# Prompt attention in a hybrid decoder step: making the next pair's queries, keys and first scores inside the running pair

## The reference, cut to what matters

```
q = (c_q @ w_q_up)                      # 512 -> 16 heads x 96, then rope on the last 32
kv = (c_kv @ w_kv_up)                   # 256 -> 16 heads x (64 keys, 64 values)
for blk in range(L // Q_BLOCK):         # 4 blocks of 128 queries
    s = (q_nope . k_nope + q_pe . k_pe) * scale
    mask = pos[q0:q1, None] >= pos[None, :q1]
    p = softmax(where(mask, s, -inf))
    outs.append(p @ v[:, :q1])
# decode: q_lat = q_nope @ w_uk; scores against a paged cache of latents and rotary keys
# S5: products of the powers of a_bar with b_bar and c, used by the chunked scan
```

## Time and profile before

| | |
|---|---|
| median of 3 runs | 1593.4 us |
| lowest, highest | 1583.5, 1593.82 us |
| profiled execution, first to last instruction | 1590.6 us |
| first query product to the last values product | 79.3 to 314.5 us |
| TensorE: busy with matmuls, with weight loads | 94%, 89% of the span |
| VectorE, ScalarE, GpSimd busy | 49%, 38%, 22% |

### The profile page before, as it was taken

The page is one execution under the profiler, slowest core; times in us unless marked ns, Lnnn a source line. Parts: engine busy times, 40 slices in busy tenths (PEclk is TensorE's granted clock), DMA queues, the critical chain, the costliest instruction groups (busy, mean ns, idle before and its releaser), DMA issues.

```text
span 1590.6 us, 32114 instructions
## 1 busy us (share of the span) xinstructions
PE 1497.3 (94%) x11463; PEld 1418.5 (89%) x11463; DVE 772.5 (49%) x1234; ACT 603.5 (38%) x1085; POOL 356.2 (22%) x422
## 2 busy tenths in 40 slices
PE   5978998889999999999999998789999999999997
PEld 5966676688887999999999998789999999999997
DVE  3876656555553543442334454964444423344332
ACT  6444545475553333311233333342333311233233
POOL 0286776344310002200022132000012200122000
PEclk9999999999999999999999999889999999999998
DMA  7123323333433123223232565512222232222321
GB/s 178 24 59 87 100 79 101 111 97 91 116 91 116 55 84 88 79 85 87 71 87 79 179 153 159 191 35 80 79 80 79 79 93 79 80 79 85 87 67 60
DMA packets 245283, 147.62 MB, mean 93 GB/s; under 512 B 42072, under 2 KB 239615, under 8 KB 244191
## 3 DMA queue, kind: packets, MB, share of 16 engines
q1 hardware_dynamic: 237826, 138.35, 30.1%
q0 software_dynamic: 6704, 7.20, 1.8%
q10 hardware_dynamic: 684, 1.18, 0.2%
HBM read 128.42 MB, written 18.26 MB: 92 GB/s over the span
## 4 chain that ended last, share of the span: by engine, by line
PE 85%; DVE 8%; ACT 3%; issue 3%; DMA 1%; SPq 0%; ACTq 0%; DVEq 0%
PE bank L856 62%; PE bank L776 7%; PE bank L1114 3%; PE bank L1079 3%; PE bank L919 2%; PE bank L979 2%; PE bank L936 1%; PE bank L967 1%; DVE arena L2050 1%; DVE tmpa L2339 1%; ACT arena L1375 1%; DVE arena L2366 1%; DVE sq L2339 1%; DVE tmpa L2048 1%; DVE tmpa L2047 1%
## 5 line engine op out<-in xcount | busy, mean ns | idle before, releaser
L856 PE MATMUL bank<-arena_parts,wR 128*128 128x288 f32 x4224 | 566.0, 296 | 4.2 <-ACT arena_parts L1452 3.7
L856 PEld LDWEIGHTS bank<-arena_parts,wR 128*128 128x128 f32 x4224 | 562.9, 188 | 5.2 <-issue 4.9
L856 PE MATMUL bank<-side_parts,wR 128*128 128x288 f32 x3360 | 447.3, 295 | 1.1 <-DVE tmpa L2411 1.1
L856 PEld LDWEIGHTS bank<-side_parts,wR 128*128 128x128 f32 x3360 | 445.5, 188 | 1.5 <-issue 1.3
L1859 DVE TENSOR_TENSOR wR<-wraw,wR 128x1024 fp32r<-128x1024 f32 x159 | 232.8, 1464 | 241.5 <-ACT wR L1438 240.1
L741 POOL TENSOR_TENSOR arena_parts<-sq,arena_parts 128x576 f32 x64 | 91.6, 1431 | 729.8 <-ACT arena_parts L1669 729.8
L1438 ACT ACTIVATE wR<-wraw 128x1024 fp32r<-128x1024 f32 x159 | 167.0, 1050 | 202.0 <-PE bank L856 187.5
L1375 ACT ACTIVATE arena<-bank 128x256 f32<-128x256 f32 (+9 forms) x223 | 95.3, 443 | 135.0 <-PE bank L776 87.9
L1666 ACT ACTIVATE tmpa<-bank 128x576 f32<-128x576 f32 x64 | 41.7, 651 | 195.5 <-PE bank L856 195.5
L2262 DVE TENSOR_TENSOR sq<-tmpa 128x576 f32<-128x576 f32 x64 | 48.5, 759 | 127.2 <-ACT tmpa L1666 127.2
L2190 DVE TENSOR_TENSOR kpR<-bank,rstd 128x576 f32<-128x576 f32 x32 | 24.2, 758 | 127.9 <-PE bank L856 127.9
(11 more groups left out here) (300 smaller groups left out, 1604.6 us busy)
## 6 DMA issues: line engine op xcount, KB each, us to landing
wraw<-in_mlp_w SPq DMA_DIRECT2D x128, 512.0 KB, 4.0
side<-in_cache_ckv SPq DMA_DIRECT2D x128, 128.0 KB, 2.1
wraw<-in_ssm_w_glu SPq DMA_DIRECT2D x16, 512.0 KB, 4.0
s_state_to_out<-side SPq DMA_DIRECT2D x16, 256.0 KB, 2.5
s_in_to_state<-yblk SPq DMA_DIRECT2D x8, 512.0 KB, 2.6
s_in_to_out<-side SPq DMA_DIRECT2D x64, 64.0 KB
wraw<-in_mla_w_o SPq DMA_DIRECT2D x8, 512.0 KB, 5.2
side<-s_in_to_state SPq DMA_DIRECT2D x2, 2048.0 KB, 13.2
```

The costliest lines, as they stand in the source:

```text
L856: return pe.matmul(bank[:, a, 0:HALF], wR[:, s, wp, k, :], tokens(k, xp)[:, a * HALF:(a + 1) * HALF], start=(first and j == 0), stop=(last ...
```

## The change

Two sets of queries and keys now exist, chosen by the parity of the pair: the second query buffer lies in `sq`, the second key buffers in `acc` and `side`. The third score bank becomes half of `bank45`, and banks 6 and 7 (`bank67`) become helpers in which everything else of a pair is made, one thing after the other. Inside pair p, TensorE now makes the query product of head 0 of pair p+1 after the values of units 0 and 1, that of head 1 after the values of units 2 and 3, the keys of p+1 after the transposes of unit 5, and the scores of units 0 and 1 of p+1 around the last transposes of p. The values product, the up-projection's transposes and the latent queries stay at the pair's start; `chunk_lags` moves from the end of pair p to the start of pair p+1. The loops take two pairs per turn, with the first and the last pair written out. The four loads of decode keys move from GpSimd's queue to the sync engine's, behind the two pages; the query weights get a load of their own, which waits until the former ones have been cut. GpSimd cuts the weights of pair p+1 at the head of its turn p. The core of the diff, TensorE first:

```diff
-        score_banks = [bank01[:, 0, :], bank01[:, 1, :], bank6[:, :]]
+        score_banks = [bank01[:, 0, :], bank01[:, 1, :], bank45[:, 1, :]]
...
+            def pair_of_heads(p, par, first=False, last=False):
+                if not first:
+                    pe.wait_ge(yt_sb, p + CREDIT)
+                    values_product()
+                    turn_up_keys(bank6)
+                unit_scores(p, par, 2)
+                unit_turn(p, 0)
+                if not first:
+                    pe.wait_ge(v_sb, p + 1)
+                    chunk_lags(p - 1)
+                latent_queries(p, par)
+                unit_scores(p, par, 3)
+                unit_turn(p, 1)
+                unit_scores(p, par, 4)
+                unit_turn(p, 2)
+                pair_values(p, 0)
+                if not last:
+                    pe.wait_ge(ql_sb, p * 4 + 4 + CREDIT)
...
+                        pe.wait_ge(kd_sb, p + CREDIT)
+                    query_product(p + 1, 0, bank67)
+                unit_scores(p, par, 5)
+                unit_turn(p, 3)
+                unit_scores(p, par, 6)
+                unit_turn(p, 4)
+                pair_values(p, 2)
+                if not last:
+                    pe.wait_ge(qn_sb, p * 2 + 3)
+                    pe.wait_ge(qr_sb, p * 2 + 3)
+                    query_product(p + 1, 1, bank67)
+                unit_scores(p, par, 7)
+                unit_turn(p, 5)
+                if not last:
+                    pe.wait_ge(qn_sb, p * 2 + 4)
+                    pe.wait_ge(qr_sb, p * 2 + 4)
+                    keys_product(p + 1)
+                unit_turn(p, 6)
+                pair_values(p, 4)
+                if not last:
+                    unit_scores(p + 1, 1 - par, 0)
+                chunk_turn(p, last)
+                unit_turn(p, 7)
+                if not last:
+                    unit_scores(p + 1, 1 - par, 1)
                 pair_values(p, 6)
```

VectorE's new order in the pair (`queries_out` is the four operations of one head, L2045 to L2050):

```diff
+            def pair_of_heads(p, par, first=False, last=False):
+                if not first:
+                    values_out(p)
+                unit_scale(p, 0)
+                unit_max(p, 2)
+                if not first:
+                    lags_out(p - 1)
+                latent_queries(p)
+                unit_scale(p, 1)
+                unit_max(p, 3)
+                unit_scale(p, 2)
+                unit_max(p, 4)
+                unit_scale(p, 3)
+                if not last:
+                    queries_out(p + 1, 1 - par, 0, bank67)
+                unit_max(p, 5)
+                unit_scale(p, 4)
+                unit_max(p, 6)
+                unit_scale(p, 5)
+                if not last:
+                    queries_out(p + 1, 1 - par, 1, bank67)
+                unit_max(p, 7)
+                unit_scale(p, 6)
+                if not last:
+                    rotary_rows(p + 1, 1 - par)
+                unit_scale(p, 7)
+                if not last:
+                    unit_max(p + 1, 0)
+                    unit_max(p + 1, 1)
```

ScalarE, GpSimd and the sync engine:

```diff
+                unit_turned(p, 0)
+                unit_exp(p, 2)
+                if not last:
+                    cut_queries_of(p + 1)
+                chunk_inputs(p)
+                unit_turned(p, 1)
...
+                unit_turned(p, 6)
+                if not last:
+                    unit_exp(p + 1, 0)
+                chunk_turned(p)
+                unit_turned(p, 7)
+                if not last:
+                    unit_exp(p + 1, 1)
                 heads_out(p)
...
-            def chunk_of_pair(p):
-                if not isinstance(p, int):
-                    rest_of_weights(p)
+            def chunk_of_pair(p, last=False):
+                if not last:
+                    rest_of_weights(p + 1)
...
+            with sp.Fori(1, PAIRS - 2) as p:
                 sp.wait_ge(uk_done, p + 1 + CREDIT)
                 apart(sp)
                 pair_weights(p + 1)
                 first_pages(p)
-                chunk_out(p)
-            first_pages(PAIRS - 1)
+                chunk_out(p - 1)
+                sp.wait_ge(wq_lo, p * 6 + 12)
+                apart(sp)
+                query_weights(p + 2)
```

More of the change, by code:

```diff
@@ L681, in chunk_of_pair @@
                 pool.tensor_tensor(CA[:, 1].rearrange("p q k o -> p (q k o)"), t[2], t[3], ALU.subtract).then_inc(ca_made, 1)
[L683 to L687, removed]
             chunk_of_pair(0)
-            with pool.Fori(1, PAIRS) as p:
+            with pool.Fori(1, PAIRS - 1) as p:
                 chunk_of_pair(p)
+            chunk_of_pair(PAIRS - 1, True)
             def load_keys(i, par):
@@ L969, in keys_product, with query_product @@
                 ins.then_inc(k_done, 1)
-            def pair_of_heads(p, last):
-                pe.wait_ge(hw_in, p * 96 + 96)
+            def query_product(p, h, banks):
                 pe.wait_ge(wq_lo, p * 6 + 6)
[L974 to L993, removed]
@@ new lines, in query_product, with values_product @@
+                for a in range(2):
+                    cols = slice(a * HALF, (a + 1) * HALF)
+                    for j, (w, x) in enumerate(((wqH, HI), (wqH, LO), (wqL, HI))):
+                        for k in range(4):
+                            ins = pe.matmul(banks[:, a, 0:HALF], w[:, k, h, :], cqH[:, k, cols] if x == HI else cq_lo[k][a],
+                                            start=(j == k == 0), stop=(j == 2 and k == 3))
+                ins.then_inc(q_done, 1)
+            def values_product():
@@ L1015, in pair_of_heads @@
                 ins.then_inc(ql_done, 1)
[L1017 to L1030, removed]
@@ new lines, in _ @@
+            for h in range(2):
+                query_product(0, h, pair[h])
+            pe.wait_ge(h_ready, H_CKV + 2)
+            pe.wait_ge(var_ready, 2)
+            keys_product(0)
+            values_product()
+            turn_up_keys(bank45[:, 0, :])
+            pe.wait_ge(kpe_raw, 1)
+            unit_scores(0, 0, 0)
+            unit_scores(0, 0, 1)
+            pair_of_heads(0, 0, first=True)
+            with pe.Fori(0, PAIRS // 2 - 1) as i:
+                pair_of_heads(i * 2 + 1, 1)
+                pair_of_heads(i * 2 + 2, 0)
@@ L1440, in cut_queries_of @@
             def cut_queries_of(p):
-                act.wait_ge(hw_in, p * 96 + 96)
+                act.wait_ge(wq_in, p * 32 + 32)
+                if not (isinstance(p, int) and p == 0):
+                    act.wait_ge(q_done, p * 2)
                 for h in range(2):
@@ L1536, in pair_of_heads, with up_keys_out @@
+            def up_keys_out(p, bank):
                 act.wait_ge(uk_done, p + 1 + CREDIT)
[L1537 to L1540, removed]
-                    unit_turned(p, u)
[L1542 to L1547, removed]
@@ L1555, in pages_turned @@
+            keys_out(0, 0)
+            up_keys_out(0, bank45[:, 0, :])
+            unit_exp(0, 0)
+            unit_exp(0, 1)
+            pair_of_heads(0, 0, first=True)
+            with act.Fori(0, PAIRS // 2 - 1) as i:
+                pair_of_heads(i * 2 + 1, 1)
+                pair_of_heads(i * 2 + 2, 0)
+            pair_of_heads(PAIRS - 1, 1, last=True)
             def pages_turned(b, par, g):
@@ L2078, in _, with pair_of_heads @@
                 dve.tensor_copy(kdc[:, P + GS:2 * P], bank7[:, GS:P]).then_inc(kd_sb, 1)
-                step.leave(PAIRS)
+            def pair_of_heads(p, par, first=False, last=False):
+                if not first:
+                    values_out(p)
+                unit_scale(p, 0)
+                unit_max(p, 2)
+                if not first:
+                    lags_out(p - 1)
[18 more added lines that the diff above has]
+                unit_scale(p, 7)
+                if not last:
+                    unit_max(p + 1, 0)
+                    unit_max(p + 1, 1)
+            for h in range(2):
+                queries_out(0, 0, h, pair[h])
+            unit_max(0, 0)
+            rotary_rows(0, 0)
+            unit_max(0, 1)
+            values_out(0)
+            pair_of_heads(0, 0, first=True)
+            with dve.Fori(0, PAIRS // 2 - 1) as i:
+                step.enter(i, 2 * (4 + 8))
+                pair_of_heads(i * 2 + 1, 1)
+                pair_of_heads(i * 2 + 2, 0)
+                step.leave(PAIRS // 2 - 1)
+            pair_of_heads(PAIRS - 1, 1, last=True)
+            lags_out(PAIRS - 1)
             dve.wait_ge(s_done, 8 * PAIRS)
```

177 lines of the change are left out of this document (107 added, 70 removed).

## The result

The changed kernel takes 1651.1 us (median of 4 runs, 1645.0 to 1654.0) against 1593.5: a ratio of 1.0377, 95% interval 1.0342 to 1.0412. Slower by 58 us, where 37 were forecast. The forecast range ended at 1652; the median lies just inside it, and 1.0377 times the 1593.4 of before, 1653.5, just outside.

What follows compares the result with a forecast made beforehand. TensorE was taken to bound the kernel. Waits of 10.1 us a pair made 33.1 us, 5.3 more than before, seven times: 1593.4 + 36.8 = 1630 us, range 1608 to 1652.

Steps and rivals of the forecast that it cites:

- The bound and its room: TensorE leads and idles 3.2 us a pair, so hiding work can win at most 26 us in all, 1.6%.
- the third: TensorE waits 1.65 us before head 0's query product for GpSimd's low part of the weights.
- the walk: Both orders timed, engine by engine: 27.8 us a pair before, 33.1 after, a difference of 5.3 us.
- The first: TensorE waits 3.3 us before unit 4's transposes, whose scaling queues behind VectorE's pass over head 0.
- the second: TensorE waits 2.7 us before the next pair's keys, for VectorE's pass over head 1.
- the sum's clock: Every item of a pair counted at its duration in a full-clock pair; nothing added for slower matmuls.
- (c): Rival: the clock falls in every pair and slows a query product, 9 to 22 us on top, 1639 to 1652; chance 0.15.
- It comes seven times: The 5.3 us surplus comes in seven of eight pairs, 37 us; the ends nearly cancel.
- The parts at nothing: Moving the decode-key loads to the sync engine is off the path; the two-pair loop costs 0 to 3 us, taken as 0.
- (a): Rival: VectorE's pass fits within TensorE's other work and the interleaving fills the idle, 1567 or about 1580; chance 0.08.
- (b): Rival: no wait for GpSimd before head 0's product, and a rotary sum of 0.75 us: 1613; chance 0.15.
- (d): Rival: the unit chain sets the pair's length either way, 1593 within 1%; chance 0.07, shared with another near-no-change case.

Runs made afterwards that it cites:

- run 6: Changed kernel with ScalarE's rounding of the next pair's query weights moved to the start of the pair: 1632.5 us, ratio 1.0266.
- run 5: Changed kernel with the helper banks released to TensorE after VectorE's second rotary multiplication, not after the rotary sum: 1640.8 us, ratio 1.0320.
- run 2: Changed kernel with VectorE's scalings of units 4 and 6 ahead of its passes over heads 0 and 1: 1618.8 us, ratio 1.0186.
- run 1: Changed kernel with unread matmuls filling TensorE's four waits of each pair: 1628.1 us, ratio 1.0248.
- run 4: Changed kernel with the loads of decode keys back on GpSimd's queue: 1649.2 us, ratio 1.0375.
- run 3: Changed kernel without the rotary multiplications and most of the rotary sum for pairs 1 to 7, shortening VectorE's pass: 1599.0 us, ratio 1.0065.
- Run 7: Changed kernel with scalings before passes, banks released before the rotary sum, query weights rounded early, unit 7 copied before S5 transposes: 1606.1 us, ratio 1.0080.
- run 8: The kernel of Run 7 with unread matmuls before the transposes of units 0 and 1, the next keys and the last values: 1585.4 us, ratio 0.9969.

## Why the prediction was wrong

**The bound and its room: right.** TensorE led with 3.2 us of idle a pair, and no run made a pair shorter than the 27.9 us of before: 28.9 without most of the pass, 28.1 repaired and filled.

**The waits: right by place and cause, and in their sum; the third came at half its size.** Forecast 3.3, 2.7 and 1.65 us; measured 4.0, 2.1 and 0.9, with 1.2 forecast and 1.0 measured at the last values. Their sum is 8.9 forecast and 8.1 measured. By the windows idle rose by 6.0 us a pair, against the 5.3 of the walk. The first is longer by the rotary sum, 1.77 us and not 1.16; run 6, where the sum took 0.75, had 3.1. Run 6 removed the third, run 5 cut the second by 0.9 us, and run 2 removed the first, of which about half came back elsewhere. With the clock held (run 1) the pair took 33.9 us against the walk's 33.1, and 1.0248 times 1593.4 is 1633 against the forecast 1630.

**The step that failed is the sum's clock.** It took every item's duration at full clock, so that the term for slower matmuls stood at nothing, and put the lower level among the rivals, (c), at 0.15 and 1.3 to 3.2 us a pair. The price was bounded by one fall in a pair that had only short waits. The row that should have raised it was in the working: a query product that meets the lower level costs up to its own length again, and the change puts both products right behind waits. What came was a fall behind the first wait in every pair, 1.0 to 2.1 us in head 1's product alone, and in five of the six pairs another, at head 0's product (1.5 us, two pairs) or at the keys (three pairs, as at 268.06): 3.6 us a pair by run 1 and by busy time, above the top of (c). Over six pairs that is 22 us, and the kernel ended 21 above the forecast, so that (c) is the rival that came. The rule of the Trainium skill ("TensorE: Matmul & The Clock Gate", section "HAM oscillation"), that idle between bursts brings the lower clock back each time, held here for the waits of 4 us, in all six pairs. For shorter waits it did not hold each time: behind the 2.1 us before the keys the clock stayed up in the pair from 202.06 and fell in the next. The fall belonged in the sum and not among the rivals.

**"It comes seven times": wrong, and hidden by the rest.** Six full pairs carried the surplus; the ends together cost 2.5 us more, not one more pair of 5.3. Of these 2.5 only 0.4 are idle: the first pair has the new stall (3.1 us), but it had waited 6.3 us for VectorE before, and the last one lost its helper work. That the shortfall of 21 us looks like the clock alone is luck: the 2.8 us too many here, and a clock fall in pair 4 of before (1.3 us), offset the idle, which was forecast 0.7 us a pair too low, 4.2 us in six.

**The parts at nothing: right.** The loads of decode keys cost nothing on either queue (run 4); no row read here shows a cost of the longer loop.

**The rivals.** (a) needed the pass under 2 us; run 3 gave it 1.1 and the pair was 28.9 us, so the interleaving doesn't fill the idle even then: other short waits (up to 0.8, 1.0, 0.9 us) are there. (b) was half seen: the third stall was 0.9, but the sum longer. (d) fell at once. The advice of the Trainium skill to interleave regimes ("Perfetto Trace Analysis", section "Optimization Strategy"), weighed in the forecast, brought no gain that a run shows: 1585.4 us with the interleaving and 1586.7 without, both with filler.

## What to carry to other kernels

Before moving a product into gaps of its engine, list what must be read out of its banks, on which in-order queue, and which scaling or maximum of the running work then stands behind it; with one set of helper banks the pass over them is serial with the product, whatever the engines' busy shares are. Price a new wait ahead of dense matmuls twice, once as the wait and once as the matmuls at the lower clock, and test it with unread matmuls in the wait: here this gave back 20 us of 58 in one edit. And put the scaling that releases TensorE ahead of a long pass in VectorE's order: by itself that gave back 30, about half of them through the clock. The two overlap in what they give back, so they don't add up to 50.

## What the hardware showed that was not expected

Waits need not be long for the clock to fall, and waits alike don't always bring it down. Ahead of head 0's product stand waits of 0.3, 0.5 and 0.9 us in the changed kernel, in every pair; the product was slow in two pairs of six. Run 6 has the 0.3 and 0.5 alone, and it was slow in none. Run 7 has the same 0.3 and 0.5, and it was slow in all six (3.7 to 5.1 us). Six unread matmuls there, with those at the keys and the last values, kept the clock up (run 8), with the transposes and latent queries between as they were. Which of these places mattered, and what differs between runs 6 and 7, was not tried.

The rotary sum, SBUF to SBUF, took 0.75 to 1.83 us: in the pair shown 0.75 in the pass over head 1, when GpSimd was idle, and 1.77 in the pass over head 0, with GpSimd's S5 products running beside it. No run parts the two.
